# Seven attention heads a layer: probabilities turned by VectorE's 32x32 blocks and DRAM transfers, value products two steps later

## The reference

```python
# a head: two 64-wide components c of q and k, one 128-wide v
s = jnp.einsum('bqhcd,bkhcd->bhcqk', qblk, kh) * scale      # q in blocks of 128
p = jax.nn.softmax(s, axis=-1)
p_diff = p[:, :, 0] - lam * p[:, :, 1]
o = jnp.einsum('bhqk,bkhv->bqhv', p_diff, vh)               # then rmsnorm, gain, gate
```

## Time and profile before

| | us |
|---|---|
| median of 3 runs | 1446.96 (1446.93 to 1447.20) |
| the profiled execution | 1447.37 |
| its span | 1445.4 |

### The profile page before, as it was taken

The page is one execution under the profiler, slowest core; times in us unless marked ns, Lnnn a source line. Parts: engine busy times, 40 slices in busy tenths (PEclk is TensorE's granted clock), DMA queues, the critical chain, the costliest instruction groups (busy, mean ns, idle before and its releaser), DMA issues.

```text
span 1445.4 us, 28896 instructions
## 1 busy us (share of the span) xinstructions
PE 1426.9 (99%) x11484; PEld 1325.2 (92%) x11484; DVE 1104.4 (76%) x1835; ACT 807.2 (56%) x1722; POOL 105.8 (7%) x110
## 2 busy tenths in 40 slices
PE   9999999999999999999999999999999999999998
PEld 8999999999999999999998888888888889999987
DVE  6988878788665777777667888888896657777765
ACT  7565555665433565656555555566654446655554
POOL 0001110001100000000000010000001000000010
PEclk9999999999999999999999999999999999999999
DMA  5222222122323322222233222222223232233332
GB/s 200 90 87 74 70 79 88 61 73 74 90 80 110 89 82 81 84 87 86 69 103 103 74 88 74 88 71 77 74 76 108 74 110 89 89 93 99 90 99 76
DMA packets 57606, 126.77 MB, mean 88 GB/s; under 512 B 7425, under 2 KB 23937, under 8 KB 57473
## 3 DMA queue, kind: packets, MB, share of 16 engines
q1 hardware_dynamic: 57472, 124.94, 27.8%
HBM read 105.77 MB, written 10.49 MB: 80 GB/s over the span
## 4 chain that ended last, share of the span: by engine, by line
PE 78%; DVE 10%; ACT 5%; issue 5%; DMA 1%; SPq 0%; DVEq 0%; ACTq 0%
PE proj L1759 54%; PE far L2015 5%; PE pair L1895 3%; PE pair L1998 3%; PE pair L2000 2%; PE far L2029 2%; PE far L2017 1%; DVE ops L1510 1%; ACT q_level L969 1%; DVE w_lo L1225 1%; ACT w_hi L812 1%; PE far L1905 1%; PE pair L1949 1%; PE far L1876 1%; PE pair L1956 1%
## 5 line engine op out<-in xcount | busy, mean ns | idle before, releaser
L1759 PE MATMUL proj<-u_hi,w_hi 128*128 128x264 f32 (+1 forms) x1960 | 485.8, 316 | 3.6 <-DVE w_lo L1225 1.9
L1759 PE MATMUL proj<-u_hi,w_lo 128*128 128x264 f32 (+1 forms) x1960 | 457.9, 302 | 0.0
L1759 PE MATMUL proj<-u_lo,w_hi 128*128 128x264 f32 (+1 forms) x1960 | 457.8, 302 | 0.0
L1759 PEld LDWEIGHTS proj<-u_hi,w_hi 128*128 128x128 f32 x1960 | 314.1, 189 | 23.4 <-DVE w_lo L1225 3.0
L1759 PEld LDWEIGHTS proj<-u_hi,w_lo 128*128 128x128 f32 x1960 | 313.7, 188 | 13.7
L1759 PEld LDWEIGHTS proj<-u_lo,w_hi 128*128 128x128 f32 x1960 | 314.0, 188 | 9.5
L1225 DVE TENSOR_TENSOR w_lo<-w_raw,w_hi 128x1024 fp32r<-128x1024 f32 x178 | 221.0, 1241 | 38.8 <-ACT w_hi L812 38.8
L1038 ACT ACTIVATE decay<-pair,neg_max 128x528 f32<-128x528 f32 (+1 forms) x144 | 100.3, 697 | 219.3 <-DVE neg_max L1614 219.2
L812 ACT ACTIVATE w_hi<-w_raw 128x1024 fp32r<-128x1024 f32 x178 | 186.5, 1048 | 41.6 <-PE proj L1759 39.1
L1614 DVE TENSOR_REDUCE neg_max<-pair 128x1 f32<-128x528 f32 (+1 forms) x144 | 101.4, 704 | 99.2 <-PE pair L2000 99.2
L969 ACT ACTIVATE q_level<-ops 128x528 f32<-128x528 f32 (+1 forms) x96 | 62.3, 649 | 78.9 <-DVE ops L1510 78.8
(11 more groups left out here) (242 smaller groups left out, 2318.1 us busy)
## 6 DMA issues: line engine op xcount, KB each, us to landing
w_raw<-w_units SPq DMA_DIRECT2D x178, 512.0 KB, 3.3
v_scratch<-v_blocks SPq DMA_DIRECT2D x128, 64.0 KB, 2.5
v_rows<-v_scratch SPq DMA_DIRECT2D x32, 256.0 KB, 3.1
q_stack<-gate_f SPq DMA_DIRECT2D x32, 132.0 KB, 2.3
k_stack<-k_stack SPq DMA_DIRECT2D x32, 132.0 KB, 2.3
h<-x_t SPq DMA_DIRECT2D x8, 264.0 KB, 5.2
cos_sin<-rope SPq DMA_DIRECT2D x2, 528.0 KB, 5.8
out_t<-ops SPq DMA_DIRECT2D x2, 512.0 KB, 3.4
```

Source lines behind the costliest of these rows:

```text
L1759: ins = pe.matmul(out, w, x[:, tile, cols_n], start=(k == 0 and p == 0), stop=(k == last_k and p == 2))
```

## The change

For heads 8 to 14 (`bounced`) and chunks of 128 queries, 56 in all, the four large transposes on TensorE and ScalarE's copy of them are left out. VectorE transposes the weighted difference in 32x32 blocks into `p_blocks`, right behind forming it; SyncE writes this to DRAM in four DMAs and reads it back in one into one of two places in `ops` (`p_rows`). The value product takes its stationary operand from there, 16 bytes from one element to the next, since the four key chunks lie interleaved. The small transpose of the meta keys stays on TensorE. The turn of chunk j moves from step 2j + 3 to 2j + 5 and its value product from 2j + 4 to 2j + 6; the 16 meta queries of layer 0 are turned in step 11 and multiplied in step 12, with places of their own in PSUM and `cols`. `row_inv` has four slots in place of two. SyncE's stacking copies are placed by step, not by unit. Head 15 is as before.

```diff
-STACK_AFTER = {FIRST_UNIT[c] + (12 if c == HG_HEADS + 1 else 6): c - HG_HEADS for c in range(HG_HEADS, HEADS)}
+def bounced(c):
+    return HG_HEADS <= c < HEADS - 1
+def turn_step(c, j):
+    if not bounced(c):
+        return 2 * j + 3
+    return 2 * j + 5 if j < N_CHUNKS else AT_STEPS - 2
+def value_step(c, j):
+    if not bounced(c):
+        return 2 * j + 4
+    return 2 * j + 6 if j < N_CHUNKS else AT_STEPS - 1
...
+        p_blocks = ops[:, 0, 0, 0:SEQ]
+        p_rows = [ops[:, 0, 1 + i, 0:SEQ].rearrange("p (n h) -> p h n", h=N_CHUNKS) for i in range(2)]
...
+            def write_probs(b):
+                sp.wait_ge(p_blocked, b + 1)
+                if b >= 2:
+                    sp.wait_ge(p_landed, 16 * (b - 1))
+                for i in range(N_BLOCKS):
+                    sp.dma_start(p_scratch[b % 2][:, i, :].rearrange("(j c) x -> c j x", j=N_BLOCKS),
+                                 p_blocks[i * BLOCK:(i + 1) * BLOCK, :].rearrange("c (j x) -> c j x", j=N_BLOCKS))\
+                        .then_inc(p_written, 16)
+            def read_probs(l, c, j):
+                b = block_of(l, c, j)
+                sp.wait_ge(p_written, 16 * N_BLOCKS * (b + 1))
+                if b >= 2:
+                    done = before(l * AT_HEADS + c - HG_HEADS, 5, AT_HEADS) + j - 1
+                    sp.wait_ge(pv_done, done if j >= 2 else done - (query_chunks(l) - N_CHUNKS))
+                sp.dma_start(ops[:, 0, 1 + b % 2, 0:SEQ],
+                             p_scratch[b % 2].rearrange("p i x -> p (i x)")).then_inc(p_landed, 16)
...
+                        for j in range(N_CHUNKS if bounced(c) else 0):
+                            if s == 2 * j + 3:
+                                write_probs(block_of(l, c, j))
+                            if s == 2 * j + 4:
+                                read_probs(l, c, j)
+                        if HG_HEADS <= c + 1 < HEADS and s == stack_steps(l, c)[1] + 1:
+                            stack_other(l * AT_HEADS + c + 1 - HG_HEADS)
...
+                    if bounced(c) and j < N_CHUNKS:
+                        b = block_of(l, c, j)
+                        dve.wait_ge(p_ready, chunks_before + j + 1)
+                        if b > 0:
+                            dve.wait_ge(p_written, 16 * N_BLOCKS * b)
+                        dve.transpose(p_blocks.rearrange("p (j r h) -> p h j r", j=N_BLOCKS, r=BLOCK),
+                                      qk_dec[:, j % 2, 0, N_META:T]
+                                      .rearrange("p (h j c) -> p h j c", h=N_CHUNKS, c=BLOCK)).then_inc(p_blocked, 1)
...
+                landed = bounced(c) and j < N_CHUNKS
+                if landed:
+                    pe.wait_ge(p_landed, 16 * (block_of(l, c, j) + 1))
+                out = attended(c, j)
+                for kk in range(4):
+                    probs = p_rows[block_of(l, c, j) % 2][:, kk, :] if landed else cols[:, kk, :]
+                    pe.matmul(out, probs, v_main(kk), start=(kk == 0), stop=False)
```

More of the change, by code:

```diff
@@ L1030, in attend @@
                 chunks, chunks_before = query_chunks(l), before(a, 5, AT_HEADS)
-                if comp == 1 and i == chunks - 1:
-                    copy_turned(a, i - 1, chunks_before)
+                early = not bounced(c) and s == 2 * chunks - 1
+                if early:
+                    copy_turned(l, c, chunks - 2)
                 if i < chunks:
@@ L1065, in attend, with take_output @@
-                if comp == 1 and 1 <= i < 1 + chunks and i != chunks - 1:
-                    copy_turned(a, i - 1, chunks_before)
+                for j in range(chunks):
+                    if s == value_step(c, j):
+                        take_output(l, c, j)
+                for j in range(chunks):
+                    if s == turn_step(c, j) and not (early and j == chunks - 2):
+                        copy_turned(l, c, j)
+            def take_output(l, c, j):
+                n, a = l * HEADS + c, l * AT_HEADS + c - HG_HEADS
+                chunks, chunks_before = query_chunks(l), before(a, 5, AT_HEADS)
+                rows = P if j < 4 else N_META
+                if j == 0:
+                    act.wait_ge(o_turned, turned(n))
+                    act.wait_ge(mix_lo_ready, n)
+                act.wait_ge(pv_done, chunks_before + j + 1)
+                inv = row_inv[0:rows, j % 4, 0:1]
+                act.activation(o_rows[0:rows, j, :], attended(c, j)[0:rows, :], ACT.Copy, scale=inv)\
+                    .then_inc(pv_read if j < chunks - 1 else o_taken, 1)
+                if j < chunks - 1:
+                    act.wait_ge(pv_read, before(a, 4, AT_HEADS) + j + 1)
+                else:
+                    act.wait_ge(o_taken, n + 1)
+                    act.wait_ge(act_step, first_squares[0])
+                act.activation(sq[0:rows, squares(j)], o_rows[0:rows, j, :], ACT.Square,
+                               accum_out=o_sums[0:rows, j:j + 1])\
+                    .then_inc(act_step if j < chunks - 1 else sq_ready, 1)
+                if j < chunks - 1:
+                    own[0] += 1
+                if j == 0:
+                    first_squares[0] = own[0]
@@ L2008, in attend @@
                     turn_meta(n - 1)
-                if comp == 0 and 2 <= i < 2 + chunks:
-                    j = i - 2
-                    pe.wait_ge(pt_ready, chunks_before + j + 1)
-                    if j == 0:
-                        pe.wait_ge(v_landed, 16 * (n + 1))
-                    for kk in range(4):
-                        pe.matmul(meta[:, 0:P], cols[:, kk, :], v_main(kk),
-                                  start=(kk == 0), stop=False)
-                    pe.matmul(meta[:, 0:P], cols[:, 4, :], v_meta[:, :],
-                              start=False, stop=True).then_inc(pv_done, 1)
@@ L2019, in attend @@
-                if comp == 1 and 1 <= i < 1 + chunks:
-                    j = i - 1
-                    rows = P if j < 4 else N_META
-                    if j == 0:
-                        pe.wait_ge(mixed, n)
-                    else:
-                        pe.wait_ge(pv_read, before(a, 4, AT_HEADS) + j)
-                    pe.wait_ge(p_ready, chunks_before + j + 1)
-                    p = qk_dec[0:rows, j % 2, 0, :]
+                for j in range(chunks):
+                    if s == value_step(c, j):
+                        times_values(l, c, j)
@@ new lines, in attend, with times_values @@
+                for j in range(chunks):
+                    if s == turn_step(c, j):
+                        turn_probs(l, c, j)
+            def times_values(l, c, j):
+                n, chunks_before = l * HEADS + c, before(l * AT_HEADS + c - HG_HEADS, 5, AT_HEADS)
+                pe.wait_ge(pt_ready, chunks_before + j + 1)
+                if j == 0:
+                    pe.wait_ge(v_landed, 16 * (n + 1))
+                landed = bounced(c) and j < N_CHUNKS
[5 more added lines that the diff above has]
+                    pe.matmul(out, probs, v_main(kk), start=(kk == 0), stop=False)
+                pe.matmul(out, cols[:, meta_cols(c, j), :], v_meta[:, :],
+                          start=False, stop=True).then_inc(pv_done, 1)
@@ new lines, in turn_probs @@
+            def turn_probs(l, c, j):
+                n, a = l * HEADS + c, l * AT_HEADS + c - HG_HEADS
+                rows = P if j < 4 else N_META
+                if j == 0:
+                    pe.wait_ge(mixed, n)
+                elif not bounced(c) or j < N_CHUNKS:
+                    pe.wait_ge(pv_read, before(a, 4, AT_HEADS) + j)
+                pe.wait_ge(p_ready, before(a, 5, AT_HEADS) + j + 1)
+                p = qk_dec[0:rows, j % 2, 0, :]
+                if not bounced(c) or j == N_CHUNKS:
@@ L2028, in attend @@
                     for kk in range(4):
                         pe.transpose(main[:, kk * P:kk * P + rows], p[:, chunk(kk)], ident[0:rows, 0:rows])
[L2030 to L2031 removed]
+                pe.transpose(meta_turned(c, j), p[:, 0:N_META], ident[0:rows, 0:rows]).then_inc(p_turned, 1)
             for l in range(DEPTH):
```

61 lines of the change are left out of this document (26 added, 35 removed).

## The result

| kernel | median us | runs |
|---|---|---|
| before | 1447.08 | 1446.93 to 1448.29 |
| after | 1512.79 | 1511.73 to 1514.68 |

The ratio is 1.0454, with a 95% interval of 1.0435 to 1.0472: the change costs 65.7 us. The forecast was 1484 in a range of 1457 to 1508, so its sign was right and its size was not: the time lies above the range.

What follows compares the result with a forecast made beforehand. TensorE, busy 1426.9 of 1445.4 us, was taken as the bound. Heads 9 to 14 at +2.6 us (layer 0) and +4.1 (layer 1), less 1.8 twice for head 8, gave +36.6 on 1447.0: 1484 us, range 1457 to 1508.

Steps and rivals of the forecast that it cites:

- The value products' weights: not in the sum: TensorE's spread weight loads: bounds of nothing and 0.11 us a load, 0.9 us a product; taken as nothing.
- rival (a): Strided weights are slow on TensorE: 0.9 us a product, +54.6 us in all, 1502 us; chance 0.22.
- The transposes removed: Four TensorE transposes gone per group, 0.44 us each group, 56 groups: 24.6 us, counting only where everything waits for TensorE.
- VectorE's transpose: 56 added ahead of the next row maximum, written 16 bytes apart: 1.05 us start to start, other bound 0.65.
- rival (b): The strides cost nothing at all, transposes at 0.65 us: +18 us, 1465 us; chance 0.15.
- The chain of maxima: Layer 0 head: added transposes delay VectorE's row maxima, step 8's to 560.05 from 558.42; the fourth transpose ends at 562.9.
- The round trip: End of a layer 0 head: probabilities' writes and read take 3.94 + 3.1 us, TensorE waits; +2.6 us a head.
- Layer 1: Heads 9 to 14 there: the last read goes out behind SyncE's stacking copies; +4.1 us a head.
- Head 8: Its steps of 6 to 8 us hide transposes and DMAs, so it gains 1.8 us a layer.
- Rival (c): All added work is hidden behind TensorE: 24.6 us come off, 1422 us; chance 0.08.
- Rival (d): DMAs crowd each other, or SyncE's waits hold a weight unit back: +23 us on the forecast, 1507 us; chance 0.07.

Runs made afterwards that it cites:

- e4: Kernel before, with only the value products' weights of heads 8 to 14, chunks 0 to 3, read 16 bytes apart from the same buffer: 1497.82 us.
- e2: Kernel after, with the value products' weights read in a row; VectorE's transposes still write 16 bytes apart: 1488.35 us.
- e8: e7 without VectorE's 56 transposes too, so nothing stands in place of TensorE's transposes: 1441.44 us.
- e3: Kernel after, with VectorE's transposes written in runs of 32 elements; weights still read 16 bytes apart: 1500.21 us.
- e5: Kernel after, with two key chunks interleaved instead of four (8-byte strides) and the read-back in two DMAs instead of one: 1479.84 us.
- e6: Kernel after, with both strides taken away: transposes written in runs of 32, weights read in a row, one read-back DMA: 1472.62 us.
- e7: e6 without the four DRAM writes and the read of each block of probabilities: 1459.80 us.
- e17: e5 with the writes and reads of the probabilities issued by GpSimd in place of SyncE: 1694.75 us.

## Why the prediction was wrong, point by point

**The step that failed** is "The value products' weights: not in the sum". It had the right end in hand, 128 x 0.83 ns = 0.11 us a load from the earlier trace rows, and took the other, "since the row of the other end is another engine's and a write". Measured are 0.12 us a load (0.23 apart in place of 0.11) and 0.91 us a product by e4, against 0.9 in the text. In the kernel after this term is 24.4 us (e2), where the sum had nothing. The two edits have the same layout, and the forecast priced them by opposite rules: VectorE's write at the strided end, TensorE's read at the contiguous one. With nothing to tell them apart, both belonged on the same side, and rival (a) was the likelier case.

**Rival (a)** had the mechanism and the price, and 1502; the time is 10.8 us above it. Of these, 6.4 us are waits that it counted on: it took 18 us for the spread weights, and they cost 24.4. In head 8 it had 3.6 us a layer (measured 3.9 and 3.6, from e2's 82.96 and 77.30 to 86.88 and 80.85). In heads 9 to 14 it put 0.9 on the path, that of step 12; between the two profiled executions (27.2 us apart in their spans) it was 2.0 in layer 0 and 1.2 in layer 1. The rows of layer 0 tell where. In e2 TensorE still waits 1.63 us ahead of step 10's product; in the kernel after, 0.26:

```profile
488.59 0.97 PEld L2115 LDWEIGHTS far<-v_rows,ops 128*128 128x128 f32 x8 [1.63 <-ACT cols L1095]
```

The maxima of step 9 start 29.98 us into e2's head (486.87) and 30.06 into after's (575.59). So the loads of steps 6 and 8 were absorbed, as (a) said. Those of step 10 were not: the wait stands ahead of that product, and behind it, up to the next head, TensorE waits 0.22 us at one place in both kernels. Steps 10 and 12 were both paid, 2 x 1.0. The other 4.35 us are the forecast's own error (e2 against 1484); in e2 six transposes of VectorE waited 5.0 us for the writes of the chunk before, a wait that the text doesn't have.

**The transposes removed, 24.6 us.** The work went, the time did not: e8 shows 6.2 us. The text had this for steps 3 and 4 ("of 1.56 us ... 1.4 turn into waiting"; 1.27 did: 5.38 us after, 5.67 before), and so the heads came out right.

**VectorE's transpose, 1.1 us.** Measured 1110 ns. The other bound, 0.65 from start to start, is what e3, e5 and e6 have (712). From e2 to e6 it is worth 15.7 us, where rival (b) gave 19 (1484 - 1465).

**The chain of maxima** held. On the clock of before (11.83 us earlier than in after's head from 545.53), VectorE's maxima:

```profile
568.19 0.71 DVE L1693 TENSOR_REDUCE neg_max<-pair 128x1 f32<-128x528 f32 x1
571.37 0.69 DVE L1693 TENSOR_REDUCE neg_max<-pair 16x1 f32<-16x528 f32 x1
```

| | forecast | measured |
|---|---|---|
| maximum of step 5 | 550.5 | 549.97 |
| maximum of step 7 | 556.8 | 556.36 |
| maximum of step 8 | 560.05 | 559.54 |
| fourth transpose ends | 562.9 | 562.6 |

**The round trip** was right in size, and wrong as a wait in layer 0. In that head the four writes go out at 574.42, the read at 579.15, 4.73 us later (3.80 in e2; forecast 3.94), and reads land in a median of 2.8 us (forecast 3.1). But TensorE doesn't wait for it in layer 0: with spread loads it starts step 12's product at 583.26, after the data. And in e2, where the forecast should hold, it waits longest ahead of step 10's product, for ScalarE's copy behind an exponential, and not in step 12 for the DMA; by that wait it comes to step 12 at 570.1 on the clock of before, where the data were forecast for 570.0. So the 40.1 us were met in part by luck, through another wait than the one named. (The terms of the text add up to 573.7 and not 573.8, 0.1 us a head.)

**Layer 1.** "The read goes out behind the stacking copies" is what the trace has, in another layer 1 head:

```profile
1312.83 1.77 SPq L784 DMA_DIRECT2D p_scratch<-ops  x4
1315.45 1.11 SPq L725 DMA_DIRECT2D q_stack<-gate_f  x2
1316.60 1.24 SPq L729 DMA_DIRECT2D k_stack<-k_stack  x2
1317.95 0.53 SPq L795 DMA_DIRECT2D ops<-p_scratch  x1
```

In e2 TensorE waits 1.2 to 2.1 us ahead of the last value product of a layer 1 head, so here the wait for the DMA is real; ahead of step 10's product it waits longer still, 2.1 us or more, for ScalarE's copy. The 38.5 us forecast are e2's shortest head; the others took 38.8 to 39.3, some of the 4.35 us.

**Head 8** is 1.77 and 1.6 us shorter in e2, where 1.8 was forecast; in the kernel after the spread loads turn that into 2.1 and 1.9 more. **Rival (c)**, all hidden, would have needed 1422. Even e8, where nothing is left to hide, takes 1441: under this order of steps it could not be reached. **Rival (d)**, DMAs that crowd each other, is not the miss: reads land in 2.8 us in the median and 4.4 at most. Weights land in 3.8 us, before in 3.3, but so they do where the trip is gone (3.7 in e7). What late transfers there are cost the kernel after 3.7 us of VectorE's time, in its five waits for the writes.

The parts in one line: before 1447.6 (beside e6 to e8), less 6.2 for TensorE's transposes, plus 18.4 for VectorE's short ones, 12.8 for the trip, and 40.2 for the two strides together (24.4 and 12.6 when taken out alone), make 1512.8.

## What to carry to other kernels

A layout that suits one engine's write is read by another, and both pay for its stride; when no row shows a strided access of the one, price it like the other. Work taken off the busiest engine counts only as far as the next engine's queue allows (here 0.3 and 0.1 of 1.76 us a head), and a wait can absorb only what stands ahead of it in its queue, so go through the costs in order and keep a balance of each wait. With 8-byte strides the same edit was a loss in six heads and a gain in the one whose steps are long enough to cover it: look for that place before giving an idea up.

## What was not expected of the hardware

- A load of 128x128 fp32 weights lasts 327 ns with 16 bytes from element to element and 192 in a row, 0.23 and 0.11 us from start to start; with 8 bytes it lasts 196.
- The 128x512 block transpose takes 1110 ns with outputs 16 bytes apart and 713 with 8.
- One DMA issue held GpSimd for 571 or 762 ns, and its transfers landed as soon as SyncE's; of two reads issued in a row the second went out when the first had landed.
- A 64 KB write to DRAM landed in 1.9 us in the median and in 4.3 at most (e6).
- With 0.71 us more in VectorE's queue, 56 times, the kernel before took 13.3 us longer, though VectorE was busy only 76% of it.

Left open are why GpSimd's second read waits for the first in e17, why some writes of the probabilities land late, and why e5 is slower than e6. Weights in contiguous runs of 32 elements, which would need no stride at all, were not tried.
